# Feed-forward of a hybrid decoder layer: the down projection by seven block products

## What is computed

```python
h2 = rms_norm(x, norm2_g[l])
x = x + (jax.nn.silu(h2 @ w_ffn_gate[l]) * (h2 @ w_ffn_up[l])) @ w_ffn_down[l]
```

## Time and profile before

| what | value |
|---|---|
| median of 3 runs | 2110.63 us (2108.84 to 2111.22) |
| the profiled execution, its own time | 2111.37 us |
| its span, first to last instruction | 2109.7 us |
| TensorE busy | 2050.8 us, 97% |
| VectorE, ScalarE, GpSimd busy | 1241.0, 688.3, 783.4 us |
| feed-forward chunk, start to start | 60.02 us, 11 of them |

### The profile page before, as it was taken

The page is one execution under the profiler, slowest core; times in us unless marked ns, Lnnn a source line. Parts: engine busy times, 40 slices in busy tenths (PEclk is TensorE's granted clock), DMA queues, the critical chain, the costliest instruction groups (busy, mean ns, idle before and its releaser), DMA issues. The chain is left out here.

```text
span 2109.7 us, 29366 instructions
## 1 busy us (share of the span) xinstructions
PE 2050.8 (97%) x9905; PEld 1674.3 (79%) x9905; DVE 1241.0 (59%) x1974; ACT 688.3 (33%) x1228; POOL 783.4 (37%) x697
## 2 busy tenths in 40 slices
PE   6999999999999999999998999988999999999999
PEld 5888888887777777777776888876888888888887
DVE  5768687743567766766756645567444444444544
ACT  4424333311334434434445100036223233322222
POOL 4413232322212211221220434358555555555552
PEclk9999999999999999999998999998999999999999
DMA  4112021223342243144354522211111111110112
GB/s 129 45 31 60 25 55 41 59 66 98 77 110 63 66 109 73 56 109 80 49 150 147 214 68 89 80 59 52 32 59 60 60 60 60 43 57 32 48 60 80
DMA packets 137744, 153.42 MB, mean 73 GB/s; under 512 B 7704, under 2 KB 112160, under 8 KB 137696
## 3 DMA queue, kind: packets, MB, share of 16 engines
q1 hardware_dynamic: 135952, 149.64, 25.8%
q10 hardware_dynamic: 1744, 3.15, 0.4%
HBM read 106.64 MB, written 20.97 MB: 60 GB/s over the span
## 5 line engine op out<-in xcount | busy, mean ns | idle before, releaser
L125 POOL TENSOR_TENSOR w_hi<-w_raw,w_ones 128x64 fp32r<-128x64 f32 x88 | 32.9, 374 | 1005.3 <-PE sb_g L151 464.1
L129 POOL TENSOR_TENSOR w_lo<-w_raw,w_hi 128x512 fp32r<-128x512 f32 x176 | 242.4, 1398 | 7.3
L813 DVE TENSOR_TENSOR sb_wt_lo<-sb_t,sb_wt_hi 128x512 fp32r<-128x512 f32 (+2 forms) x186 | 103.0, 554 | 113.2 <-ACT sb_wt_hi L634 111.3
L151 PE MATMUL sb_g<-h_hi,w_hi 128*128 128x512 f32 x544 | 153.0, 409 | 2.7 <-DVEq L693 1.9
L151 PE MATMUL sb_g<-h_lo,w_hi 128*128 128x512 f32 x544 | 150.6, 401 | 0.0
L151 PE MATMUL sb_g<-h_hi,w_lo 128*128 128x512 f32 x544 | 150.3, 400 | 0.0
L634 ACT CAST sb_wt_hi<-sb_t 128x512 fp32r<-128x512 f32 (+2 forms) x186 | 89.7, 482 | 166.6 <-PE sb_t L500 166.0
L2076 POOL TENSOR_TENSOR ff_w_lo<-raw_g,ff_w_hi 128x512 fp32r<-128x512 f32 x66 | 85.6, 1297 | 109.5 <-ACT ff_w_hi L2192 109.5
L151 PE MATMUL gla_g<-h_hi,w_hi 128*128 128x512 f32 x464 | 124.0, 402 | 0.0
L151 PE MATMUL gla_g<-h_lo,w_hi 128*128 128x512 f32 x464 | 122.8, 397 | 0.0
L151 PE MATMUL gla_g<-h_hi,w_lo 128*128 128x512 f32 x464 | 122.5, 397 | 0.0
(11 more groups left out here) (406 smaller groups left out, 4948.5 us busy)
## 6 DMA issues: line engine op xcount, KB each, us to landing
w_raw<-w_in SPq DMA_DIRECT2D x64, 512.0 KB, 8.1
raw_g<-w_ffn_gate SPq DMA_DIRECT2D x11, 1024.0 KB, 5.2
ff_raw_u<-w_ffn_up SPq DMA_DIRECT2D x11, 1024.0 KB, 5.7
ff_raw_d<-w_ffn_down SPq DMA_DIRECT2D x11, 1024.0 KB, 4.7
sb_qs<-sb_q_st SPq DMA_DIRECT2D x32, 256.0 KB, 5.1
sb_kh<-sb_k_st SPq DMA_DIRECT2D x32, 256.0 KB, 5.0
sb_kl<-sb_k_st SPq DMA_DIRECT2D x32, 256.0 KB, 5.0
mp_sig<-gates_t SPq DMA_DIRECT2D x16, 512.0 KB, 4.2
```

The lines of the kernel that those rows point to most:

```text
L125: self.nc.gpsimd.tensor_tensor(hi[:, 0:64], raw[:, 0:64], self.ones[:], ALU.mult)
L129: ins = self.nc.gpsimd.tensor_tensor(lo[:, at], raw[:, at], hi[:, at], ALU.subtract)
L151: ins = nc.tensor.matmul(acc, a[:, k, :], b[:, k, half * HALF:(half + 1) * HALF], start=(n == 0), stop=(n == len(steps) - 1))
L813: nc.vector.tensor_tensor(wt_lo[:, m % 2, a:HALF], weight_bank(m, last)[:, a:HALF], wt_hi[:, m % 2, a:HALF], ALU.subtract).then_inc(lo_rea ...
```

## The change

The block of hidden activations (two halves of 128 columns by two halves of 512 rows) times the rows of w_ffn_down (two halves of rows by two halves of columns) is 8 block products of 4 groups of 3 matmuls. The change computes it from 7, P1 to P7 in the order D_ORDER. P1 uses the first quadrant and P2 the fourth gated one (u_12) as they are, P4 the third; the others use sums of quadrants and sums of weight blocks. Products are chained in two sets of four banks (DX: P1, P6, P7, P4, each adding to what is there; DY: P2, then P5 and P3), and after each block the banks are added into one quarter of y, so that VectorE adds 28 times. Weight sums (down_sum) go to GpSimd; of the activation sums two go to VectorE (y_sum_1, y_sum_2), two to GpSimd (y_sum). They are made behind the last gated quadrant. PE's second block is P2, the last quadrant. RING goes from 6 to 4 slots, with the buffers of the down part laid over one another; GpSimd's first gate and up sums come behind P2's low parts, the later behind P5's; the load of down rows waits for the end of the down part. The core of the diff:

```diff
-    RING = 6
+    RING = 4
     NP = 14
-    ND = TT * NH
     PP = TT // 2
-    SLOTS_PER = NP + 4
+    NG = TT // 2
+    ND = 7 * NG
+    SLOTS_PER = NP + 7
     ROOT_CHAIN = 12
     P1, P2, P3, P5, P6, P7, P4 = range(7)
     ORDER = (P1, P2, P5, P3, P6, P7, P4)
+    D_ORDER = (P1, P2, P6, P5, P7, P3, P4)
     G, U = 0, 1
...
-        down = [E[0], E[1], A[0], A[1]]
+        DX = [Y[0], Y[1], E[0], E[1]]
+        DY = [X[0], X[1], A[0], A[1]]
...
+        D_CHAIN = {P1: DX, P6: DX, P7: DX, P4: DX, P5: DY, P3: DY, P2: DY}
+        D_BLOCK = {P1: (0, 0), P2: (0, 0), P6: (0, 1), P3: (0, 1), P5: (1, 1), P7: (1, 1), P4: (1, 0)}
+        Y_HIGH = {P1: 1, P5: 2, P2: 3, P6: 4, P4: 5, P7: 6, P3: 7}
...
+        b = [[block_of(raw_d, f, nh) for nh in range(NH)] for f in range(2)]
+        B_AT = {P1: (0, 0), P5: (0, 0), P4: (1, 0), P7: (0, 1), P2: (1, 0), P3: (1, 1)}
+
+        def down_operand(j):
+            if D_ORDER[j] == P6:
+                return w_sum[:]
+            f, nh = B_AT[D_ORDER[j]]
+            return b[f][nh]
+
+        assert (NP + D_ORDER.index(P6)) % RING == 0
+
+        def down_slot(j):
+
+            if D_ORDER[j] == P4:
+                return block_of(last_d, 0, 0), block_of(last_d, 1, 0)
+            return w_hi[ring(j)][:], w_lo[ring(j)][:]
+
+        def d_read(j, g, ch):
+            return 4 + ND * ch + NG * j + g + 1
+
...
-                    sp.wait_ge(w_ready, d_first(ch) + 4)
+                    sp.wait_ge(d_done, ND * ch + ND)
                     load_down(ch * PAIR + PAIR)
...
+                for j in (1, 4, 5, 6):
+                    for g in range(NG):
+                        mi, nh = D_BLOCK[D_ORDER[j]]
+                        t, cols = NG * mi + g, slice(nh * HALF, (nh + 1) * HALF)
+                        sp.wait_ge(d_free, d_read(j, g, N - 1))
+                        sp.dma_start(out[t * P:(t + 1) * P, cols], y[:, t, cols]).then_inc(out_done, 16)
...
                 def gate_up(ch, slot, at):
-                    for m in (G, U):
-                        sums_1(m, ch)
                     for n, p in enumerate(ORDER):
                         for m in (G, U):
                             low(slot(2 * n + m), m, p, at + 2 * n + m + 1)
                         if p == P2:
+                            for m in (G, U):
+                                sums_1(m, ch)
+                        if p == P5:
                             for m in (G, U):
                                 sum_2(m, ch, at)
                             for m in (G, U):
...
+                def down_low(j, ch):
+                    pool.wait_ge(w_high, d_first(ch) + j + 1)
+                    hi, lo = down_slot(j)
+                    nc.gpsimd.tensor_tensor(lo, down_operand(j), hi, ALU.subtract).then_inc(w_ready, 1)
+
+                def down_sum(n, ch, lows, dst, left, right):
+
+                    pool.wait_ge(w_ready, d_first(ch) + lows)
+                    need(pool, b_made, 4 * ch + n if n else 0)
+                    nc.gpsimd.tensor_tensor(dst, left, right, ALU.subtract).then_inc(b_made, 1)
...
+                def y_sum(p, ch):
+                    if p == P3:
+                        pool.wait_ge(y_ready, 4 * ch + 4)
+                    pool.wait_ge(y_summed, 2 * ch + 2)
+                    nc.gpsimd.tensor_tensor(y_raw[p], u[3] if p == P3 else u[2], y_raw[P6], ALU.subtract
+                                            ).then_inc(y_summed_pool, 1)
...
+                def y_low_pool_part(p, ch):
+                    pool.wait_ge(y_high, 7 * ch + Y_HIGH[p])
...
+                    nc.gpsimd.tensor_tensor(y_lo[p][:], y_raw[p], y_hi[p][:], ALU.subtract).then_inc(y_low_pool, 1)
+
+                def down_block(ch):
+                    (b11, b12), (b21, b22) = b
+                    down_low(0, ch)
+                    down_sum(0, ch, 1, b11, b12, b11)
+                    down_low(1, ch)
+                    pool.wait_ge(gu_done, NP * ch + NP - 1)
+                    down_sum(1, ch, 1, w_sum[:], b22, b11)
+                    down_sum(2, ch, 2, b21, b21, w_sum[:])
+                    down_low(2, ch)
+                    down_sum(3, ch, 1, b12, b22, b12)
+                    down_low(3, ch)
+                    y_sum(P7, ch)
+                    down_low(4, ch)
+                    y_low_pool_part(P7, ch)
+                    y_sum(P3, ch)
+                    down_low(5, ch)
+                    y_low_pool_part(P3, ch)
+                    down_low(6, ch)
+                    y_low_pool_part(P4, ch)
...
+                def down_high(j, ch):
+                    p = D_ORDER[j]
+                    if p in (P1, P2, P3):
+                        act.wait_ge(raw_loaded[2], 16 * ch + 16)
+                    else:
+                        act.wait_ge(b_made, 4 * ch + {P5: 1, P6: 2, P4: 3, P7: 4}[p])
+                    if p == P4:
+                        act.wait_ge(w_ready, d_first(ch) + 4)
+                    nc.scalar.copy(down_slot(j)[0], down_operand(j)).then_inc(w_high, 1)
...
+                def y_round(p, ch):
+                    if p in (P1, P2, P4):
+                        act.wait_ge(y_ready, 4 * ch + {P1: 1, P2: 4, P4: 3}[p])
+                    elif p in (P7, P3):
+                        act.wait_ge(y_summed_pool, 2 * ch + {P7: 1, P3: 2}[p])
+                    else:
+                        act.wait_ge(y_summed, 2 * ch + {P5: 1, P6: 2}[p])
+                    nc.scalar.copy(y_hi[p][:], y_raw[p]).then_inc(y_high, 1)
+
+                def down_block(ch):
+                    y_round(P5, ch)
+                    y_round(P2, ch)
+                    y_round(P6, ch)
+                    act.wait_ge(d_done, ND * ch + NG)
+                    down_high(4, ch)
+                    y_round(P4, ch)
+                    act.wait_ge(d_done, ND * ch + 2 * NG)
+                    down_high(5, ch)
+                    y_round(P7, ch)
+                    down_high(6, ch)
...
@@ -2219,28 +2325,23 @@
                         if i == 4:
                             sigmoid(0, ch)
                         if i == 5:
-                            y_round(0, ch)
+                            y_round(P1, ch)
...
                         if i == 10:
                             sigmoid(1, ch)
-                            y_round(1, ch)
+                        if i == 12:
+                            sigmoid(3, ch)
+                        if i + RING >= NP:
+                            down_high(i + RING - NP, ch)
                         if i == 11:
                             sigmoid(2, ch)
-                        if i < 8:
-                            high(slot(i + 6), i + 6, ch)
-                        elif i < 12:
-                            down_high(i - 8, ch)
-                        if i == 12:
-                            y_round(2, ch)
-                            sigmoid(3, ch)
-                        if i == 13:
-                            y_round(3, ch)
+                        if made <= i < NP - RING:
+                            high(slot(i + RING), i + RING, ch)
...
+                    down_block(ch)
+                    for n in range(RING):
+                        act.wait_ge(d_done, ND * ch + NG * (n + 3))
+                        high(n, n, ch + 1)
+                        if n == 0:
+                            y_round(P3, ch)
+                    gate_up(ch + 1, lambda n: n % RING)
+                down_block(N - 1)
+                y_round(P3, N - 1)
...
+                def y_low_part(p, ch):
+                    dve.wait_ge(y_high, 7 * ch + Y_HIGH[p])
+                    if p == P5:
+                        dve.wait_ge(y_summed, 2 * ch + 2)
+                    tt(y_lo[p][:], y_raw[p], y_hi[p][:], ALU.subtract).then_inc(y_low, 1)
+
+                def y_sum_1(ch):
+                    dve.wait_ge(y_ready, 4 * ch + 3)
+                    tt(y_raw[P5], u[1], u[2], ALU.add).then_inc(y_summed, 1)
+
+                def y_sum_2(ch):
+                    dve.wait_ge(y_low, 4 * ch + 1)
+                    dve.wait_ge(y_summed, 2 * ch + 1)
+                    tt(y_raw[P6], y_raw[P5], u[0], ALU.subtract).then_inc(y_summed, 1)
...
                     dve.wait_ge(sig_ready, 4 * ch + q + 1)
-                    tt(u[C_UP[q]][:], u[C_UP[q]][:], cg[C_GATE[q]][:], ALU.mult).then_inc(y_ready, 1)
+                    tt(u[q], u[q], cg[C_GATE[q]], ALU.mult).then_inc(y_ready, 1)
...
                     hidden(2, ch)
-                    y_low_part(2, ch)
...
+                def add(j, g, ch):
+                    p = D_ORDER[j]
+                    mi, nh = D_BLOCK[p]
+                    at = y[:, NG * mi + g, nh * HALF:(nh + 1) * HALF]
+                    dve.wait_ge(d_done, ND * ch + NG * j + g + 1)
+                    if p in (P2, P7):
+                        dve.wait_ge(d_free, d_read(j - 1, g, ch))
+                    tt(at, D_CHAIN[p][g][:], at, ALU.add).then_inc(d_free, 1)
 
                 def down_block(ch):
```

(88 more changed lines are left out.)

103 lines of the change are left out of this document (43 added, 60 removed).

## The result

| | before | after |
|---|---|---|
| median | 2110.53 us (2108.53 to 2112.07, 15 runs) | 2115.51 us (2113.28 to 2117.72, 15 runs) |
| profiled execution, its span | 2111.37, 2109.7 | 2115.73, 2113.9 |
| last down part: start, last add, end of the span | 2084.45, 2106.53, 2109.66 | 2086.11, 2109.80, 2113.90 |

A forecast was written before the change was run, and what follows sets the result against it. TensorE, busy 97% of the span, was taken to bound the kernel. From 2111.37 us, -0.4 for down parts and +0.5 for the tail gave 2111.4; with the median 0.74 lower, the forecast was 2110.7, range 2094 to 2125.

The forecast's parts named there:

- What bounds, and the matmuls taken out: TensorE bounds, 0.2267 us per matmul; 12 fewer per chunk could give 2.72 us, 29.9 us in 11 chunks, if nothing waits.
- The blocking: VectorE instructions with both inputs in SBUF do not run beside GpSimd; where both have a queue, they alternate.
- No blocking: Rival, chance 0.06: VectorE's sums do not block; P2 starts at 3.46, P6 without a wait; -22 us, 2088.
- The sign that all sums and low parts would read 1.3 to 1.8: Sign of being right: VectorE sums and low parts of 1.3 to 1.8 us instead of 0.69.
- The walk: Timeline through one down block: PE loses 1.7 us before P2, 0.8 before P6; down part 21.90 for 21.94, -0.4 in all.
- Ring, loads, GpSimd's margins: Four weight slots for six and the later down load cost nothing; GpSimd's later low parts arrive before they are needed.
- P6's low part misses its turn: Slower rival, chance 0.18: in the down part PE begins P6 1.25 us later; +13 us, 2124.
- Both places go to VectorE: Faster rival, chance 0.16: VectorE wins both contested turns, at P2 and P6; down part 20.64, -14 us, 2096.
- The first activation sum misses its turn: Rival, chance 0.10, margin 0.2 us: P2 starts at 5.83, P6 without a wait; down part 22.25, +3.4 us, 2114.
- The clock: Rival, chance 0.03: PE's idle times lower the granted clock, 10 us at half clock losing 5 us per chunk; 2166.
- the tail: At the kernel's end, twelve stores 0.68 us apart before the last one crowd: +0.5 us, bounds 0 and 2.
- The sum: 2111.37 - 0.4 + 0.5 = 2111.4 us; the median of runs lies 0.74 lower, so forecast 2110.7.

The follow-up runs named there:

- runs 1 to 3: Each against after: GpSimd's fourth weight sum held until P2's low part, 2101.09 us; ScalarE rounds P2 before P5, 2099.58; GpSimd's down-weight work mostly cut to 16 columns, 2094.39.
- run 9: The kernel after, with the four adds of the first down block cut to 16 columns in the last chunk alone; 2114.81 us.
- run 6: The kernel after, with P6's low part placed behind the third add of P1 instead of the second; 2127.42 us.
- runs 2 and 4: Each against after: ScalarE rounds P2 before P5, 2099.58 us; VectorE's first sum before the last gated product, both low parts before the adds, 2096.64 us.
- run 11: After with VectorE's sums and low parts reordered, plus GpSimd held at its third low part in the last chunk alone; 2094.73 us, beside 2096.18 without the hold.
- p6_low_late: The same as run 6: the kernel after with P6's low part one add later; 2127.42 us.
- after_4stores: The kernel after with the first 12 of its 16 output stores left out; 2113.35 us.
- tail_short_adds: The same as run 9: the kernel after with four adds cut to 16 columns in the last chunk; 2114.81 us.
- before_idle: The kernel before, with one PE idle time put into every down part by waiting for the fourth quadrant's low part; 2132.49 us.

## Why the prediction was right, and where it was off

- **What bounds, and the matmuls taken out: right.** A matmul costs 0.2267 us, 84 per chunk.
- **The blocking: right.** GpSimd and VectorE take turns. Of the 2.4 us that PE waited per chunk, runs 1 to 3 put some 1.6 to these turns and 0.7 to the chain's own length. *No blocking* fell: P2's low part took 1.71 and the second sum 1.77. The sign that all sums and low parts would read 1.3 to 1.8 was too wide: the first sum and P6's low part met a GpSimd operation near its end and read 0.69 and 0.81, though they ended where the walk had them (1.59 for 1.58, 8.14 for 8.15).
- **The walk: right to 0.1 us.** P2 4.64 for 4.58, P6 8.27 for 8.20, next P1 22.00 for 21.90. The part of it most in doubt, GpSimd winning by 0.11, came as walked, by 0.10. With steps of the walk off by up to 0.1, that this one fell right is in part luck. The forecast "-0.04 per chunk" was +0.05: in before the first down matmul starts 0.05 late, and after has no such gap at its first but a longer one at each of its two restarts.
- **Ring, loads, GpSimd's margins: right.** The gate and up part takes 38.08, and GpSimd's low parts for P7, P3, P4 and the seventh of gate and up end at 11.1, 14.9, 17.4 and 36.8, as walked. In one chunk of run 9 P5's low part lost a tie by 0.01 us (GpSimd at 1613.26, VectorE at 1613.27), was stretched to 1.84, and PE waited 0.45 at P5's banks, where the prediction had a margin of 0.4:

```profile
1613.26 1.30 POOL L2204 TENSOR_TENSOR ff_s_lo<-ff_s,ff_y_hi 128x512 fp32r<-128x512 f32 x1
1613.27 1.84 DVE L2432 TENSOR_TENSOR ff_u_lo<-ff_u,ff_y_hi 128x512 fp32r<-128x512 f32 x1
1615.76 0.50 PE L2603 MATMUL ff_x_g<-ff_w_hi,ff_y_hi 128*128 128x512 f32 x1 [0.45 <-DVE y L2495]
```

- **The rivals.** *P6's low part misses its turn* did not come by itself, but forced, in run 6, it gave 2127.4 for the 2124 worked out, 12 above after where 13 above the forecast was priced. *Both places go to VectorE* (2096) did not come either; with the turns won by other means, in runs 2 and 4, the kernel took 2099.6 (PE still waits 0.48 at P6) and 2096.6. *The first activation sum misses its turn* did not come: it ended at 1.59.
- **The clock: mis-sized.** I priced it as all or nothing, 5 us in every chunk at a chance of 0.03, from one idle time of 1.83 us that did no harm. It fell behind 3 of 11 idle times, for some eight matmuls each: 0.7 to 0.8 us each time, some +2.2 on the span.
- **The step that failed: the tail.** "The store behind the last add ends the kernel ... I take +0.5 us, bounds 0 and 2." It measured 2.6: 27.79 us from the start of the last down part to the end, for 25.21 before. I priced the stores alone, and those at the pace of PE, which run 11 shows to cost about 0.1. The number needed stood in my own walk: "adds of block 2 begin at 9.8". I used it for the banks that PE waits for and did not carry it to the end: 9.8 + 23 x 0.6 = 23.6, while in before the last add starts at 22.08. That is +1.6, and by adds that run back to back the stores come closer than PE makes tiles, another 1.0.
- **The sum** forecast -0.4 + 0.5 = +0.1; the trace has +1.66 for the start of the last down part and 1.61 + 0.97 for the tail, +4.2. Of the 4.1 missed, the tail is 2.1, the clock 2.2 and the walk 1.0 (0.6 for -0.4); the early start of the first down part, which is not shown to be the change's doing, takes 1.2 off. So that the traced span comes within 4.2 is in part luck. The result lies at the bound of 0.2%: 0.23%, with an interval that reaches to both sides of it, so the cases for slower (0.28) and for within 0.2% (0.40) are told apart by little.

## What to carry to other kernels

Where two engines block each other (here GpSimd, and VectorE with both inputs in SBUF), cost an operation by the turn it gets and not by its own length: write down who asks when, to 0.1 us, and if a small margin decides, make it sure by order (cast the needed operand first, sum ahead of the wait) before paying for it with a wait. Then follow the backlog of every engine to the end of the kernel: an engine that merely "keeps ahead of the banks" in the loop ends behind, and the last store pays all of it.

## What was not expected of the hardware

- The turns are kept strictly: an instruction that asks 0.6 us later waits for one more of the other engine's and is 1.23 us late (run 6); a lead of 0.10 us, once even 0.01, decides (after; run 9). The Trainium skill, "SBUF — State Buffer", section "Who interferes with whom", says that the issue order decides who blocks and that an instruction with two inputs in SBUF meets a reading GpSimd one; the stretched rows here agree, and the adds of 512 columns, with one input in PSUM, stayed at 0.67 to 0.69.
- Idle times of PE of 1.76 to 1.83 us at P2 were followed by a lower granted clock in 6 of 44 chunks (3 in after, 2 in p6_low_late, its first and last chunk, 1 in after_4stores, none in tail_short_adds). The nine of 1.83 to 1.85 at P6 in p6_low_late, each 3 us behind one of 1.76, were followed by none, nor were those of 1.64 in before_idle or those of up to 0.94 in the other runs. Why those six is open; it wasn't tried. The last one, in p6_low_late (columns as in the earlier trace rows):

```profile
2100.00:2105.00 5.00, 4.19 (x12) 2.86 (x12) 5.00 (x6) 1.66 (x3) 4.35 (x4) 0.73 0.00 0
```

- VectorE's adds, recorded at 0.67 to 0.69 us, follow each other at 0.598 when they never wait, so its pace is about a tenth better than the records say.
